# Second attention layer: the output's factor from one minus the block's sum of weights

## The reference, cut to what matters

```python
z = jnp.einsum('bqhd,bkhd->bhqk', qb, kf) * (B_DH ** -0.5)
log_keep = jnp.where(valid, jax.nn.log_sigmoid(-z), 0.0)
after = lax.cumsum(log_keep, axis=3, reverse=True) - log_keep
a = jnp.where(valid, jnp.exp(jax.nn.log_sigmoid(z) + after), 0.0)
return jnp.einsum('bhqk,bkhd->bqhd', a, vf)
```

## Time and profile before

| | |
|---|---|
| time, median of 3 runs | 1990.98 us (1990.57 to 1994.24) |
| span of the profiled execution | 1986.7 us, so at least 3.9 us of a time lie around the span |
| PE busy | 1859.7 us, 94% of the span |
| DVE, ACT, POOL busy | 1151.5, 1031.0, 387.6 us |
| second attention layer | about 962 to 1745 us of the span |

### The profile page before, as it was taken

The page is one execution under the profiler, slowest core; times in us unless marked ns, Lnnn a source line. Parts: engine busy times, 40 slices in busy tenths (PEclk is TensorE's granted clock), DMA queues, the critical chain, the costliest instruction groups (busy, mean ns, idle before and its releaser), DMA issues. The chain is left out here.

```text
span 1986.7 us, 31724 instructions
## 1 busy us (share of the span) xinstructions
PE 1859.7 (94%) x11429; PEld 1615.1 (81%) x11429; DVE 1151.5 (58%) x2317; ACT 1031.0 (52%) x2452; POOL 387.6 (20%) x597
## 2 busy tenths in 40 slices
PE   4999999999999899999699999999999999899996
PEld 3888878888788779999587888888888888689995
DVE  5456465574555642355257667676767575844545
ACT  5355454564545532354256656575757575822345
POOL 0132231322313100156101010111111111200441
PEclk7999999999999999999799999999999999999999
DMA  4121112211122143221110202111112021242113
GB/s 155 45 79 38 49 49 60 65 39 49 49 60 65 44 152 90 65 73 59 60 39 22 65 28 70 38 50 39 55 33 60 28 60 49 77 135 90 54 54 127
DMA packets 161803, 125.07 MB, mean 63 GB/s; under 512 B 10992, under 2 KB 152624, under 8 KB 161648
## 3 DMA queue, kind: packets, MB, share of 16 engines
q1 hardware_dynamic: 160784, 122.85, 20.2%
q10 hardware_dynamic: 864, 0.20, 0.1%
HBM read 89.49 MB, written 33.52 MB: 62 GB/s over the span
## 5 line engine op out<-in xcount | busy, mean ns | idle before, releaser
L107 PE MATMUL pj<-h_high,area 128*128 128x384 f32 (+1 forms) x1536 | 380.4, 333 | 18.2 <-issue 5.8
L107 PE MATMUL pj<-area,h_high 128*128 128x384 f32 (+1 forms) x1152 | 333.0, 352 | 6.3 <-issue 5.5
L107 PEld LDWEIGHTS pj<-h_high,area 128*128 128x128 f32 x1536 | 271.0, 192 | 23.7 <-issue 11.1
L107 PE MATMUL pj<-h_low,area 128*128 128x384 f32 (+1 forms) x768 | 251.7, 328 | 0.0
L107 PEld LDWEIGHTS pj<-area,h_high 128*128 128x128 f32 (+1 forms) x1152 | 204.0, 181 | 18.6 <-issue 5.5
L1208 ACT ACTIVATE lb_m<-lb_sc 128x512 f32<-128x512 f32 (+4 forms) x200 | 88.5, 486 | 227.1 <-PE lb_sc L1642 196.3
L107 PE MATMUL pj<-area,h_low 128*128 128x384 f32 (+1 forms) x576 | 195.3, 339 | 0.0
L1557 POOL TENSOR_TENSOR lb_o<-lb_o,lb_keep 128x512 f32<-128x512 f32 (+3 forms) x80 | 77.6, 970 | 572.5 <-ACT lb_keep L1237 565.9
L1396 DVE SCALAR_TENSOR_TENSOR lb_s<-lb_sc,lb_m 128x512 f32<-128x512 f32 (+4 forms) x200 | 109.9, 549 | 69.0 <-ACT lb_m L1218 69.0
L107 PEld LDWEIGHTS pj<-h_low,area 128*128 128x128 f32 x768 | 147.6, 192 | 0.0
L455 ACT ACTIVATE la_p<-la_sc,la_nm 128x128 f32<-128x128 f32 (+5 forms) x144 | 105.8, 737 | 33.8 <-DVE la_nm L652 32.9
(11 more groups left out here) (310 smaller groups left out, 4394.2 us busy)
## 6 DMA issues: line engine op xcount, KB each, us to landing
stage<-in_a_w_in SPq DMA_DIRECT2D x60, 192.0 KB, 3.2
stage<-in_b_w_in SPq DMA_DIRECT2D x60, 192.0 KB, 3.2
stage<-in_ple_w_gate SPq DMA_DIRECT2D x22, 512.0 KB, 3.8
h_low<-o_t SPq DMA_DIRECT2D x14, 528.0 KB, 6.4
mix_b_xs<-x_mid SPq DMA_DIRECT2D x8, 528.0 KB
lift_xt<-in_x SPq DMA_DIRECT2D x8, 512.0 KB, 4.6
stage<-in_a_w_in SPq DMA_DIRECT2D x16, 256.0 KB, 5.0
out_ak<-la_tok SPq DMA_DIRECT2D x8, 512.0 KB, 3.3
```

Source lines behind the costliest of these rows:

```text
L107: last = pe.matmul(out, x, y, start=start and n == 0, stop=stop and n == 2, **kw)
```

## The change

Each head's values in `tok` get 64 columns of ones beside them: `[values of head 0 | ones | values of head 1]`. One matmul of 128 columns gives a head's values and, 64 times over, its sum of weights. Head 0 writes `acc` (values above, sums below), head 1 writes `third` (sums above, values below). ACT's factor is now 1 - sum, two instructions of 64 partitions, one from each bank. It can be had only when `values` has run, so `keep`, `scale` and `add` each move one step later, DVE's `add` is two instructions, and `column_sums` with its four matmuls a pair goes. Pairs of block 0 and the sample's pair keep their 64-wide matmuls into `acc`. The values are stored to `v_out` by two transfers of 64 features a head in place of one of 128.

```diff
-        tok = sb("tok", [P, NT + 1, 2 * P])
+        tok = sb("tok", [P, NT + 1, 3 * P])
...
-                for n, out in ((1, k_out), (2, v_out)):
...
+                for out, first, n, at_ in ((k_out, 0, P, 0), (v_out, 0, DH, P), (v_out, DH, DH, 2 * P)):
...
                 def keep(i):
                     n, q = carried(i), span(*PAIRS[i])[0]
-                    act.wait_ge(S["sums"], at.next("sums"))
+                    act.wait_ge(S["pv"], at.nth("pv", i + 1))
...
-                    act.activation(kept[n % 2][:, q:], third[:, q:], ACT.Exp).then_inc(S["keep"], 1)
+                    act.activation(kept[n % 2][0:DH, q:], acc[DH:, q:], ACT.Copy, scale=-1.0, bias=1.0)
+                    act.activation(kept[n % 2][DH:, q:], third[0:DH, q:], ACT.Copy, scale=-1.0,
+                                   bias=1.0).then_inc(S["keep"], 1)
...
+                    if i >= 2 and PAIRS[i - 2][1] > 0:
+                        keep(i - 2)
                     if i >= 1:
                         for s in units(i - 1):
                             weights(s)
-                        if PAIRS[i - 1][1] > 0:
-                            keep(i - 1)
...
-                    out = o[:, c0 + q:c0 + cn]
-                    dve.tensor_tensor(out, acc[:, q:], out, ALU.add).then_inc(S["added"], 1)
+                    upper, lower = o[0:DH, c0 + q:c0 + cn], o[DH:, c0 + q:c0 + cn]
+                    dve.tensor_tensor(upper, acc[0:DH, q:], upper, ALU.add)
+                    dve.tensor_tensor(lower, third[DH:, q:], lower, ALU.add).then_inc(S["added"], 1)
...
                 for i in range(NP + 1):
-                    if i >= 2:
-                        add(i - 2)
+                    if i >= 3:
+                        add(i - 3)
...
+                add(NP - 2)
                 add(NP - 1)
...
-                    if PAIRS[i - 1][1] > 0:
-                        scale(i - 1)
+                    if i >= 2 and PAIRS[i - 2][1] > 0:
+                        scale(i - 2)
...
+                scale(NP - 1)
...
-                def column_sums(i):
...
+                    elif b == 0:
...
                     else:
                         q = span(c, b)[0]
                         for s in units(i):
                             hd = UNITS[s][2]
-                            last = pe.matmul(acc[hd * DH:(hd + 1) * DH, q:],
-                                             tok[:, b, P + hd * DH:P + (hd + 1) * DH],
-                                             a_[s % 4][:, q:], start=True, stop=True, skip_group_check=True)
+                            last = pe.matmul((acc, third)[hd][:, q:], tok[:, b, P + hd * DH:2 * P + hd * DH],
+                                             a_[s % 4][:, q:], start=True, stop=True)
...
-                        if PAIRS[i - 1][1] > 0:
-                            column_sums(i - 1)
```

More of the change, by code:

```diff
@@ L1042, in stick_layer @@
                      turned=6, tok_ready=6, past_turned=1, past_high=1, past_low=1,
-                     tok_stored=64, g_ready=3, g_normed=3, g_clamped=3, g_exp=3, g_log=3, g_soft=3, g_sig=3, g_done=3,
-                     z=N, size=N, exp=N, log=N, soft=N, high=SPLIT, low=SPLIT, after=N, a=N, sums=CARRIED,
+                     tok_stored=96, g_ready=3, g_normed=3, g_clamped=3, g_exp=3, g_log=3, g_soft=3, g_sig=3, g_done=3,
+                     z=N, size=N, exp=N, log=N, soft=N, high=SPLIT, low=SPLIT, after=N, a=N,
                      keep=CARRIED, scaled=CARRIED, added=NP - 1, sampled=1, pv=NP, dve_link=4, o_ready=3,
@@ L1147, in body @@
                 sp.wait_ge(S["tok_ready"], at.all("tok_ready"))
-                for n, out in ((1, k_out), (2, v_out)):
[L1149 to L1153, removed]
+                for out, first, n, at_ in ((k_out, 0, P, 0), (v_out, 0, DH, P), (v_out, DH, DH, 2 * P)):
+                    sp.dma_start(out[0:SEQ, bass.ds(r * P + first, n)].rearrange("(t p) f -> p t f", p=P),
+                                 tok[:, 0:NT, at_:at_ + n]).then_inc(S["tok_stored"], 16)
+                    sp.dma_start(out[SEQ:ROWS, bass.ds(r * P + first, n)],
+                                 tok[0:DEC, NT, at_:at_ + n]).then_inc(S["tok_stored"], 16)
                 if more:
@@ L1190, in tokens @@
             def tokens(at, x):
-                p, f = x // 3, slice((kind(x) - 1) * P, kind(x) * P)
+                p = x // 3
                 act.wait_ge(S["turned"], at.nth("turned", kv_nth(x)))
                 turned = pj[:, x % 2, 0:3 * P].rearrange("p (a n) -> p a n", n=P)
+                if kind(x) == 1:
+                    placed = lambda rows, t: tok[rows, t, 0:P]
+                else:
+                    turned = turned.rearrange("p a (h n) -> p a h n", n=DH)
+                    placed = lambda rows, t: tok[rows, t, P:].rearrange("p t (h n) -> p t h n", n=P)[:, :, :, 0:DH]
+                last = slice(NT, NT + 1)
                 if p < 2:
-                    act.activation(tok[:, 3 * p:3 * p + 3, f], turned, ACT.Copy).then_inc(S["tok_ready"], 1)
+                    act.activation(placed(slice(0, P), slice(3 * p, 3 * p + 3)), turned, ACT.Copy).then_inc(S["tok_ready"], 1)
                 else:
-                    act.activation(tok[:, 6:8, f], turned[:, 0:2, :], ACT.Copy)
-                    act.activation(tok[0:DEC, NT, f], turned[0:DEC, 2, :], ACT.Copy).then_inc(S["tok_ready"], 1)
+                    act.activation(placed(slice(0, P), slice(6, 8)), turned[:, 0:2], ACT.Copy)
+                    act.activation(placed(slice(0, DEC), last), turned[0:DEC, 2:3], ACT.Copy).then_inc(S["tok_ready"], 1)
             def body(r, more):
@@ L1316, in body @@
                             next_tokens(4)
+                keep(NP - 1)
                 if not more:
@@ L1347, in _ @@
             dve.tensor_copy(tri[:, :], masks["neg_tri"][:, :])
[L1348 to L1351, removed]
+            dve.memset(tok[:, 0:NT, P + DH:2 * P], 1.0)
             dve.drain().then_inc(S["fill"], 1)
@@ L1673, in after @@
                     last.then_inc(S["after"], 1)
-                def column_sums(i):
[L1676 to L1684, removed]
                 def values(i):
                     c, b = PAIRS[i]
+                    if carried(i) == 1:
+                        pe.wait_ge(S["past_low"], at.all("past_low"))
                     pe.wait_ge(S["a"], at.nth("a", through(i)))
@@ L1704, in values @@
                                                  stop=b == PB, skip_group_check=True)
+                    elif b == 0:
+                        for s in units(i):
+                            hd = UNITS[s][2]
+                            last = pe.matmul(acc[hd * DH:(hd + 1) * DH, :], tok[:, b, (1 + hd) * P:(1 + hd) * P + DH],
+                                             a_[s % 4][:, :], start=True, stop=True, skip_group_check=True)
                     else:
@@ L1759, in body @@
                         pe.wait_ge(S["past"], at.nth("past", 32))
-                        pe.wait_ge(S["keep"], at.before("keep"))
+                        pe.wait_ge(S["added"], at.before("added"))
                         for b in range(PB):
```

7 lines of the change are left out of this document (2 added, 5 removed).

## The result

| | before | after |
|---|---|---|
| time, median | 1990.78 us (4 runs, 1989.71 to 1994.24) | 2103.62 us (4 runs, 2102.97 to 2107.69) |
| span of the profiled execution | 1986.7 us | 2101.1 us |
| ratio | | 1.0574, interval 1.0558 to 1.0589 |

The change makes the kernel 5.7% slower. The forecast was 2089 us, the range 2035 to 2135.

The account below looks back on a forecast made before the run. PE was taken to bound the kernel, losing whatever it waits. Steady groups 7*(13.7 - 2.0) = 82, last group + 8, clock + 8 gave +98 us: span 2085, median 2089 us, range 2035 to 2135.

Parts of the forecast that it names:

- What bounds the kernel: Second attention layer: PE, busy 48.48 of 48.90 us of a steady group, sets the time; waits lose it.
- The coincidence of DVE's add and PE's values: Step 8: DVE comes to pair i-2's `add` about when PE has its values (from 1429.81, `add` from 1431.50).
- PE's work: Matmuls of a group: sums dropped, value matmuls widened, together -2.0 us a group (bounds -0.9 and -3), -16 us in all.
- The stops: Steady group: PE's values wait for DVE's moved `add`, 13.7 us a group (8.2 + 5.0 + 0.5; bounds nothing and 20).
- The seven places: Steps 3, 4, 9 to 12 and the group's last values: PE waits for `slot_norm` and both add halves, 8.2 us.
- The places where DVE is behind with its own work: Steps 6 to 8 of a group: DVE reaches the add or copy late, 2.2, 0.7 and 2.1 us, together 5.0.
- The last group: Group without projections: DVE its limit; 4 us in steps 3 to 6, 0.6 per later step, 1.2 tail; +8 us.
- The clock: Granted clock falls after some PE stops of 1 us or more, 1.7 us lost each time; +8 us.
- The rest at nothing: ACT's two-instruction factors, the second v transfer and writing the ones cost nothing.
- The sum: Whole kernel: 7*(13.7 - 2.0) = 82, + 8, + 8 = +98 us; span 2085, median 2089.
- The rival of a clock that falls at most stops: Three in four of 64 stops cost 1.7 us of clock: +74 instead of +8, 2162 us; chance 0.1.
- DVE arrives in time: DVE, busy 34.52 of 48.90 us, may run ahead; only PE's saving shows, -16 us, 1975; chance 0.07.

Follow-up runs that it names:

- the kernel with the early add: Changed kernel with carried pairs' adds right behind DVE's splits, pairs without a factor added at the start of the step: 1985.72 us, ratio 0.9975.
- The early add: Changed kernel with pair i-2 added right behind the splits of pair i, in the last group alone: 2092.14 us, ratio 1.0502.
- the old way: Kernel of 1985.72 us with the last group as before the change (sums, 64-wide values, old `keep`, `scale` and `add`): 1981.48 us, ratio 0.9962.
- the kernel of 1985.72 us: Changed kernel with carried pairs' adds right behind DVE's splits, pairs without a factor added at the start of the step: ratio 0.9975.
- the run with the early `add`: Changed kernel with every add of pair i-2 right behind DVE's softplus and splits of pair i, in all groups: 2015.12 us, ratio 1.0127.

## Why the prediction was right, and where it was not

**What bounds the kernel.** Right. PE sets a steady group's time. Sparing it the sums brought 41.6 us; making it wait for the add cost 79.1. The coincidence of DVE's add and PE's values was the point: with the add late alone, the waits come to 79.2 us and the span grows by 77.0. PE is busy for 89.45 of 104.97 us of an undisturbed group, 85%, so the sign that was to refute the prediction, 98%, did not come.

**PE's work.** -2.0 us a group was predicted, -2.8 measured, inside the bounds of -0.9 to -3. Its parts: the sums 6.4 against 6.1, the widening 4.5 (5.5 less the 1.0 for the `after` matmuls) against 4.0. Whether the first layer's 0.88 ns a column was too much isn't settled: a wide pair of 1.70 us for 4*512 columns is 0.83 ns, one of 1.80 us is 0.88. By the factor of "up to 2x" in the Trainium skill, "TensorEngine Tiling (Array Packing)", Theoretical Speedup, the widening would, as an estimate, cost up to 7.1 us a group. The run with wide values shows 4.0, and the pair 1.01 us against 1.70 to 1.80, so the measurement decides against the full factor of two here.

**The stops.** 13.7 us a group predicted. The gaps in which PE waits for an add or copy in one undisturbed group after are, in order, 0.58, 1.23, 2.49, 0.99, 1.41, 1.09, 1.14, 1.32, 1.38, 0.98 and 1.51 us: 14.1. Step by step:

| step | predicted | measured |
|---|---|---|
| 3, 4 | 0.7, 1.2 | 0.58, 1.23 |
| 6, 7, 8 | 2.2, 0.7, 2.1 | 2.49, 0.99, 1.41 |
| 9, 10, 11, 12 | 1.0, 1.1, 1.3, 1.4 | 1.09, 1.14, 1.32, 1.38 |
| 5, 13, group's last | 0.1, 0.4, 1.5 | none, 0.98, 1.51 |

The seven places where the wait is `slot_norm` and two halves were right to 0.12 us, since every link was read from a row. The places where DVE is behind with its own work were right only in sum (5.0 against 4.89). For step 6 the terms as written (1.25 to DVE free, 0.5, 0.5 and 0.15) add up to 2.4, not 2.2. Step 13 was mis-sized: step 12's stop doesn't cover it. By experiment the stops are 104.97 - 92.03 = 12.9 us, the kernel with the early add still keeping some 0.7 us a group of waits for adds.

**The last group.** Mis-sized, the largest miss: +8 predicted, +23.8 measured. "DVE is its limit" failed: DVE is busy for 60.5 of 100.4 us there, and was for 59.8 of 76.7. The price of 0.6 us for each of the seven later steps failed with it: PE's stops for an add or copy there are 4.66, 0.92, 3.20, 2.26, 2.67, 2.74 and 2.89 us, 19.3 together. Most of it is again the place of the `add`: late alone it costs the group 17.0 us, with seven such stops of 16.7 us together. Here is one step of the last group after:

```profile
1818.55 2.05 PE L1710 MATMUL lb_acc<-lb_a,lb_tok 128*128 128x512 f32 x2 [3.20 <-DVE lb_o L1449]
...
1822.34 0.59 ACT L1241 ACTIVATE lb_keep<-lb_acc 64x512 f32<-64x512 f32 x1 [3.81 <-PE lb_third L1710]
...
1823.56 1.09 ACT L1232 ACTIVATE lb_a<-lb_sc 128x512 f32<-128x512 f32 x2
...
1824.54 1.08 ACT L1297 ACTIVATE h_high<-h_low 128x1056 fp32r<-128x1056 f32 x1
...
1825.65 1.26 DVE L1504 TENSOR_TENSOR h_low<-h_low,h_high 128x1056 fp32r<-128x1056 f32 x1 [3.41 <-ACT h_high L1297]
1826.83 0.68 DVE L1448 TENSOR_TENSOR lb_o<-lb_acc,lb_o 64x512 f32<-64x512 f32 x1
```

It is a ring. PE's values wait for DVE's add; the add stands behind a split of an output block (L1504), which waits for ACT's copy of it (L1297); ACT does that behind factor and weights; the factor waits for the values, and the weights for the `after` matmuls that PE runs behind the values. The ring closes through the weights even without the new factor. The kernel with the late `add` alone has it, with the old factor: values at 1788.40, weights at 1790.52, ACT's copy at 1793.57, DVE's split at 1794.68 after a wait of 1.95 us for it, add at 1795.86, values at 1796.69. Before, the add that the values ask for was a step older, so the ring had a step of slack. DVE is idle for 3.41 us of this step of 9.8. Two things in it are not the ring: PE ran at half clock at its start (granted clock 0.50 over the 5 us from 1818.55; the matmuls into `acc` and `third` start 1.84 us apart, 0.94 at 1274.38), and the 3.20 us ahead of it had DVE at work without a pause from 1811.14.

The early add takes 13.5 us off the group. With pairs without a factor added at once it takes 84.9 us, and the old way 76.6 (before 76.7). The 8.2 us between these last two go with the new factor and what it brings, the later scale and the halved add in its other place, since without sums and with wide values the group takes 74.0 us (both together), so PE's changed work is not the cause. The granted clock takes a share as well, 0.84 in the window after against 0.94 before; how large it is was not measured.

**The clock.** +8 predicted. From the periods: 1.6 + 4.3 + 1.6 + 4.3 + 1.6 = 13.4 us over 105.0 each, less before's 3.0, so +10.4 in the seven steady groups. The +8 was meant for all eight groups; what the clock costs the last one is part of its 23.8. The size was near by luck: it came from two falls after fifteen stops of about 1.2 and 1.7 us, and in the steady groups after none of the many stops of about 1.2 us was followed by one. The fifteen also left out the stop of 1.37 us in the last group before (PE at 1703.73), with a clock of 0.71 behind it. The rival of a clock that falls at most stops failed; it fell after 7 of some 70. The rule cited beside it (the Trainium skill, "TensorE: Matmul & The Clock Gate", "A second HAM failure mode: psum-queue depth-cycling"), that frequent short idles make the clock swing, isn't borne out as a forecast: more than sixty short stops of the changed kernel had no fall behind them. In the run with wide values five of seven stops of 1.18 us had one.

**The rest at nothing.** ACT's factors and the halved add cost up to 1.3 us a steady group, found by comparing 92.0 with 90.7. They are not covered in the last one. The second v transfer shows nowhere: the DMA share of a steady group is 0.14 of its time.

**The sum.** 7*(13.7 - 2.0) + 8 + 8 = 98 was predicted, 114.4 came. Steady groups without clock 7*(105.0 - 93.5) = 80.5 (82 predicted), clock 10.4 (8), last group 23.8 (8). Two terms held, one was a third of its size. The step from span to median was too large: the time of an execution lies 1.7 to 2.5 us above its span (2102.97 and 2101.1 for the profiled one after), not at least 3.9 as the table before has it, and the median after stands 2.5 above that span, not 4.3.

**Rivals.** "DVE arrives in time" failed though DVE was busy for 68 of 105 us: it arrives by its order, not by its load. The same load with the add at another place of DVE's order costs nothing, which the kernel of 1985.72 us shows. "Half the stops" failed by the table above.

## What to carry to other kernels

When a change makes an operation wait for a later producer, the buffer it frees comes free later too: look who refills that buffer, and count the step from its last reader's place in the in-order queue, not from its engine's busy share. If the reader must move, put it directly behind the last work that its engine owes the bound engine, ahead of what only prepares the next round, and leave at the front those readers that need not wait. A chain over several engines can close to a ring by a reader that stands too late in its queue as well as by a new dependence. With the add early, the new dependence cost at most 1.3 us in a group where the bound engine had filler work, and 8.2 us in the one where it had little, so the last iteration needs its own reading.

## What was not expected of the hardware

In the changed kernel the granted clock seemed to answer to a stop's length; the other kernels don't bear it out. Windows of 5 us from the end of a stop, after (granted clock is the third figure from the end):

```profile
1152.50:1157.50 5.00, 5.00 (x16) 3.39 (x17) 2.50 (x4) 1.47 (x4) 0.00 (x0) 0.50 0.00 0
1261.83:1266.83 5.00, 5.00 (x30) 3.71 (x30) 4.30 (x7) 2.40 (x6) 0.88 (x1) 1.00 0.00 0
...
1488.77:1493.77 5.00, 5.00 (x12) 3.09 (x13) 3.53 (x6) 3.18 (x7) 0.86 (x1) 0.66 0.02 3
```

The stops before them were 2.48, 2.49 and 2.10 us. In the seven steady periods there are seven stops of 2.5 us, five followed by a fall of the clock to half (1.2 GHz of 2.4 GHz), and two of 2.10 us, both followed by one. Of the other stops of 0.96 to 1.51 us there, more than sixty, none was. Yet before, two of the seven of 1.18 us in steady groups were, one of them in the earlier trace rows. In the run with wide values it was five of the same seven, the last five, each like this one:

```profile
1304.84:1309.84 5.00, 5.00 (x25) 4.87 (x26) 3.46 (x8) 2.11 (x5) 0.00 (x0) 0.66 0.02 5
```

In the run with the early `add` it was one of its seven stops of 2.4 us (clock 0.50 from 1530.52). So a stop's length alone does not decide, and what does stays open. A group with one fall costs 1.6 us more, with two 4.3.

The prediction had this, and it is worth keeping: an instruction of 64 partitions cost DVE and ACT here what one of 128 did. DVE's half adds took 0.68 and 0.69 us for 512 columns, the whole one 0.68. ACT's half factor took 0.59 us (at 1822.34, above), the whole one before, which is an exponential and not a copy, 0.60 (at 1710.10). A result spread over two banks, so that each instruction touches half the partitions, is paid for twice when it is read.
